# Turning the normed q heads with VectorE instead of TensorE in a one-core decoder layer

## The reference

```python
q, k, v = jnp.split(h @ w_in, 3, axis=-1)
q = rms_norm(split_heads(q, SB_HEADS, SB_HEAD_DIM), q_gain).astype(jnp.float32)
k = rms_norm(split_heads(k, SB_HEADS, SB_HEAD_DIM), k_gain).astype(jnp.float32)
v = split_heads(v, SB_HEADS, SB_HEAD_DIM).astype(jnp.float32)
q = q * (SB_HEAD_DIM ** -0.5)
...
z = jnp.einsum('bhqd,bhkd->bhqk', qb, k)
```

## Time and profile before

| | before |
|---|---|
| median of 3 runs | 1232.27 us |
| profiled execution | 1231.01 us |
| its span | 1229.3 us |
| PE busy | 1221.0 us (99%) |
| DVE busy | 816.4 us (66%) |
| ACT busy | 623.2 us (51%) |
| POOL busy | 79.5 us (6%) |
| granted TensorE clock | 1.00 of full speed in the attention groups |

### The profile page before, as it was taken

One profiled execution on the slowest core, in us unless ns is written; L12 is line 12 of the kernel. 1 busy time (PEld: TensorE's weight loads), 2 busy tenths in 40 slices (PEclk: granted clock), 3 DMA queues, 4 the chain that ended last, 5 costly groups with the idle time before them and its releaser, 6 DMA issues.

```text
span 1229.3 us, 17127 instructions
## 1 busy us (share of the span) xinstructions
PE 1221.0 (99%) x5552; PEld 1013.5 (82%) x5552; DVE 816.4 (66%) x1039; ACT 623.2 (51%) x741; POOL 79.5 (6%) x126
## 2 busy tenths in 40 slices
PE   8999999999999999999999999999999999999998
PEld 7888888888888788888888888888888888888886
DVE  6667577675679866765776676587665656665554
ACT  5458486584945544444444443444444444444443
POOL 0312103121001200000000000000000000002000
PEclk9999999999999999999999999999999999999999
DMA  8655554555555766666666666666565656574674
GB/s 266 204 160 168 171 171 155 179 159 155 172 169 160 220 185 201 193 184 192 203 189 185 205 190 186 200 194 178 190 211 169 213 168 219 164 223 154 198 225 133
DMA packets 120468, 229.33 MB, mean 187 GB/s; under 512 B 7490, under 2 KB 9844, under 8 KB 120436
## 3 DMA queue, kind: packets, MB, share of 16 engines
q1 hardware_dynamic: 119252, 226.80, 59.7%
q10 hardware_dynamic: 1184, 2.11, 0.5%
HBM read 226.78 MB, written 2.10 MB: 186 GB/s over the span
## 4 chain that ended last, share of the span: by engine, by line
PE 98%; DMA 0%; DVE 0%; ACT 0%; issue 0%; SPq 0%; ACTq 0%; DVEq 0%
PE acc L960 95%; PE T L974 1%; PE T L988 1%; PE Z L988 1%; PE R L1011 1%; DMA x<-in_x 0%; PE acc L1072 0%; PE Z L1001 0%; ACT w_hi L406 0%; PE R L1012 0%; DVE stage L924 0%; DVE x L927 0%; DVE neg_log_1m L697 0%; ACT softplus L474 0%; ACT softplus L472 0%
## 5 line engine op out<-in xcount | busy, mean ns | idle before, releaser
L406 ACT ACTIVATE w_hi<-raw 128x1024 fp32r<-128x1024 f32 (+1 forms) x448 | 455.1, 1021 | 523.8 <-PE acc L960 492.3
L644 DVE TENSOR_TENSOR w_lo<-raw,w_hi 128x1024 fp32r<-128x1024 f32 (+1 forms) x448 | 526.5, 1183 | 285.4 <-ACT w_hi L406 279.7
L960 PE MATMUL acc<-w_hi,xT_hi 128*128 128x512 f32 x1216 | 476.9, 392 | 0.2
L960 PE MATMUL acc<-w_hi,xT_lo 128*128 128x512 f32 x1216 | 473.7, 390 | 0.0
L960 PE MATMUL acc<-w_lo,xT_hi 128*128 128x512 f32 x1216 | 473.1, 389 | 0.0
L960 PEld LDWEIGHTS acc<-w_hi,xT_lo 128*128 128x128 f32 x1216 | 228.2, 188 | 48.0
L960 PEld LDWEIGHTS acc<-w_hi,xT_hi 128*128 128x128 f32 x1216 | 228.3, 188 | 46.9 <-issue 1.0
L960 PEld LDWEIGHTS acc<-w_lo,xT_hi 128*128 128x128 f32 x1216 | 228.4, 188 | 46.5
L960 PE MATMUL acc<-w_hi,hT_hi 128*128 128x512 f32 x352 | 136.9, 389 | 0.0
L960 PE MATMUL acc<-w_lo,hT_hi 128*128 128x512 f32 x352 | 136.9, 389 | 0.0
L960 PE MATMUL acc<-w_hi,hT_lo 128*128 128x512 f32 x352 | 136.9, 389 | 0.0
(11 more groups left out here) (124 smaller groups left out, 662.9 us busy)
## 6 DMA issues: line engine op xcount, KB each, us to landing
raw<-in_sb_w_in SPq DMA_DIRECT2D x96, 512.0 KB, 3.7
raw<-in_ffn_w_gate SPq DMA_DIRECT2D x88, 512.0 KB, 3.8
raw<-in_ffn_w_up SPq DMA_DIRECT2D x88, 512.0 KB, 3.8
raw<-in_ffn_w_down SPq DMA_DIRECT2D x80, 512.0 KB, 4.8
raw<-in_sb_w_out SPq DMA_DIRECT2D x32, 512.0 KB, 3.9
raw<-in_ple_w_gate SPq DMA_DIRECT2D x20, 512.0 KB, 4.9
raw<-in_ple_w_gate SPq DMA_DIRECT2D x24, 256.0 KB, 3.5
raw<-in_ffn_w_down SPq DMA_DIRECT2D x16, 256.0 KB, 3.1
```

What stands on the lines that cost most here:

```text
L406: act.activation(w_parts[0][:, slot(u), 0:n, :], raw[:, slot(u), 0:n, :], ACT.Copy).then_inc(hi_ready, 1)
L644: dve.tensor_tensor(w_parts[1][:, slot(u), 0:n, :], raw[:, slot(u), 0:n, :], w_parts[0][:, slot(u), 0:n, :].bitcast(F32), ALU.subtract).th ...
L960: last = pe.matmul(acc[pair][tb][:, :], parts[a][:, c, tb * P:(tb + 1) * P], w_parts[w][:, slot(u), i, :], start=(start and i == 0 and n = ...
```

## The change

The normed q heads no longer go through PE. At u = 14 to 17 DVE turns them itself, four 32x32-block instructions behind each lo, sixteen a group, into a new buffer `q_side` in SBUF; each covers all four heads and both token blocks (eight 32x32 blocks). At u = 18, behind the squares of k, ACT copies `q_side` with the gain to `qT_hi` in one instruction; at u = 19 DVE makes `qT_lo` in one instruction. The k heads stay as they were, and the counts of turn rounds in the waits are lowered from four to two a group. `norm_heads` waits for `q_side_ready` as well, and `scores` for `qT_ready`.

```diff
-    SETS0 = X_ROUNDS + 4 * GROUPS
-    SETS0_T0, SETS0_T1 = (X_ROUNDS + 1) // 2 + 4 * GROUPS, X_ROUNDS // 2
+    SETS0 = X_ROUNDS + 2 * GROUPS
+    SETS0_T0, SETS0_T1 = (X_ROUNDS + 1) // 2 + 2 * GROUPS, X_ROUNDS // 2
+    Q_TURN, Q_UNITS, Q_HI, Q_LO = 14, 4, 18, 19
+            q_side = at_row("q_side", [P, HG, SEQ])
@@ ACT, group
                         if u == end + 3:
                             square_heads(U0 + end, 3 * g + part, 2 * g + part, part)
-                        if u == end + 8:
-                            turn_heads(to, gain, 4 * g + 2 * part, 0)
-
-                        if u == min(end + 10, AU - 1):
-                            turn_heads(to, gain, 4 * g + 2 * part + 1, 1)
+                    if u == Q_HI:
+                        act.wait_ge(q_side_ready, g + 1)
+                        act.activation(qT[0][:, :, :], q_side[:, :, :], ACT.Copy, scale=gains[:, QG:QG + 1]).then_inc(q_hi_ready, 1)
+                    if u == AU - 1:
+                        turn_heads(kT, KG, 2 * g, 0)
+                        turn_heads(kT, KG, 2 * g + 1, 1)
@@ DVE
+            def turn_q(g, i):
+
+                if i == 0:
+                    left(dve, 0, A_P0 + 2 * g + 1)
+                    dve.wait_ge(qT_ready, g)
+                for a, b in QUADRANTS[i * QN * QN // Q_UNITS:(i + 1) * QN * QN // Q_UNITS]:
+                    last = dve.transpose(
+                        q_side[b * Q:(b + 1) * Q, :, :].rearrange("p h (t s) -> p t h s", t=TB)[:, :, :, a * Q:(a + 1) * Q],
+                        normed[a * Q:(a + 1) * Q, :, :].rearrange("p t (h d) -> p t h d", d=HD)[:, :, :, b * Q:(b + 1) * Q])
+                if i == Q_UNITS - 1:
+                    last.then_inc(q_side_ready, 1)
@@ DVE, group
                         if u == end + 6:
-                            norm_heads(2 * g + part, part, 4 * g + 2 * part)
-                        if u == end + 8:
-                            turn_heads(to, gain, 4 * g + 2 * part, 0)
-
-                        if u == min(end + 10, AU - 1):
-                            turn_heads(to, gain, 4 * g + 2 * part + 1, 1)
+                            norm_heads(2 * g + part, part, 2 * g, g + part)
+                    if Q_TURN <= u < Q_TURN + Q_UNITS:
+                        turn_q(g, u - Q_TURN)
+                    if u == Q_LO:
+                        dve.wait_ge(q_hi_ready, g + 1)
+                        dve.scalar_tensor_tensor(out=qT[1][:, :, :], in0=q_side[:, :, :], scalar=gains[:, QG:QG + 1],
+                                                 in1=qT[0][:, :, :].bitcast(F32), op0=ALU.mult,
+                                                 op1=ALU.subtract).then_inc(qT_ready, 1)
+                    if u == AU - 1:
+                        turn_heads(kT, KG, 2 * g, 0)
+                        turn_heads(kT, KG, 2 * g + 1, 1)
@@ PE, group
-                    for i in range(2):
-                        for m in range(2):
-                            if u == (i + 1) * DU + 4 + 2 * m:
-                                left(pe, i, (A_P0 + 2 * g, A_P1 + g)[i] + 1)
-                                turn(0, normed, 2 * m, (X_ROUNDS + 1) // 2 + 4 * g + 2 * i + m)
+                    for m in range(2):
+                        if u == 2 * DU + 4 + 2 * m:
+                            left(pe, 1, A_P1 + g + 1)
+                            turn(0, normed, 2 * m, (X_ROUNDS + 1) // 2 + 2 * g + m)
```

More of the change, by code:

```diff
@@ L203, in trunk @@
         turned_hi = sem("turned_hi")
+        q_side_ready = sem("q_side_ready")
+        q_hi_ready = sem("q_hi_ready")
+        qT_ready = sem("qT_ready")
         side_ready = sem("side_ready")
@@ L513, in group @@
                         attend(u, g - 1, A_EVERY)
-                    for part, (to, gain) in enumerate(((qT, QG), (kT, KG))):
+                    for part in range(2):
                         end = (part + 1) * DU - 1
@@ L665, in sum_heads, with norm_heads @@
                                AX_X).then_inc(head_ssq_ready, 1)
-            def norm_heads(n, pair, rounds):
+            def norm_heads(n, pair, rounds, q_turned):
                 dve.wait_ge(head_scale_ready, n + 1)
                 dve.wait_ge(T_ready, X_ROUNDS + rounds)
+                dve.wait_ge(q_side_ready, q_turned)
                 for tb in range(TB):
@@ L992, in scores @@
             def scores(h, i, g):
-                left_T0 = (X_ROUNDS + 1) // 2 + 4 * (g + 1)
+                left_T0 = (X_ROUNDS + 1) // 2 + 2 * (g + 1)
                 pe.wait_ge(T_free[0], left_T0)
+                pe.wait_ge(qT_ready, g + 1)
                 pe.wait_ge(z_free, h)
```

## The result

| | before | changed |
|---|---|---|
| median, first session (10 and 10 runs) | 1232.1 us (1231.57 to 1233.06) | 1235.9 us (1233.71 to 1238.98) |
| median, second session (16 and 11 runs) | 1232.0 us | 1234.33 us (1232.34 to 1236.53) |
| span of the profiled execution | 1229.3 us | 1234.2 us |
| granted clock of that execution | 0.999 | 0.998 |
| DVE busy | 816.4 us | 842.6 us |

The changed kernel is slower: 1.0032 of before with an interval of 1.0024 to 1.0041 in the first session, 1.0018 (1.0009 to 1.0027) in the second.

The account below looks back on a forecast made before the run. PE was taken to bound the kernel, with 98% of the chain of waits. Losses at the k turn of 1.2 + 3 × 1.6, after PE's saving, gave 6.1 us: 1237.1 profiled, 1238.4 median, range 1230.5 to 1241.

Parts of the forecast that it names:

- My own case: k chain: POOL, held by DVE's row, makes PE wait at the k turn; 6.0 to 6.1 us slower, chance 0.70.
- rival 2: k chain: DVE less late, POOL held once, turn 0.6 us late; 1231.0 us, no change that can be told; chance 0.11.
- PE's rounds: On PE: eight turn rounds go, saving 3.65 us, at least 2.9 and at most 3.9.
- DVE's backlog: DVE, third group: sixteen turns, 7.6 us a group, make `sum_heads` of k start at 211.42, hidden from PE until there.
- POOL held by the row: k chain on POOL: first small operation slips in before `qT_lo`, the second is held by the closed DVE row until 217.5.
- the case I gave beside mine: POOL gets one operation in at each row boundary; k turn at 222.4, 1.2 us lost a group, 4.7 in all.
- The first group: First group's k turn: power held until the lo of u = 21 ends, turn at 70.6 to 70.8; 1.2 us lost.
- The other groups: k turn of the three later groups: PE waits 2.5 us, its saving of 0.89 gone, 1.6 us lost each.
- The sum: Whole kernel: 1.2 + 3 × 1.6 = 6.0 to 6.1 us slower, all else hanging on PE.
- the fall of the clock: Rival 3: clock falls while PE waits, or block turns are dearer and PE waits for lo's; above 1241 us; chance 0.05.
- The signs: Expected in the profile after: second small POOL operation 3 to 4 us, PE waiting 2 to 2.5 us at four k turns.
- Rival 1: k chain: POOL is not held by the row, PE does not wait; 1228.6 us, faster; chance 0.14.

Follow-up runs that it names:

- e5: The changed kernel with one block turn a group instead of sixteen and `qT_lo` made at u = 22: 1227.55 us, 0.9964 of before.
- e2: The changed kernel with `qT_lo` at u = 22 and an idle one-input sum over `q_side` at u = 19: 1227.63 us, 0.9964 of before.
- e10: The changed kernel itself, run again with nothing altered: 1234.33 us, 1.0018 of before.
- e8: The changed kernel with turns at u = 14, 15, 16, 19, `qT_hi` at u = 20, `qT_lo` at u = 22: 1227.78 us, 0.9968 of before.
- e1: The changed kernel with `qT_lo` made at u = 22 instead of u = 19, all sixteen turns kept: 1228.38 us, 0.9967 of before.
- e4: The changed kernel with `qT_lo` made twice in a row at u = 19: 1235.44 us, 1.0032 of before.
- e7: The kernel before with two more powers in POOL's chain for the k factors: 1239.65 us, 1.0063 of before.
- e9: The kernel before with three more powers in POOL's chain for the k factors: 1255.96 us, 1.0180 of before.

## Why the prediction was right, and where its sizes were off

The forecast was slower, 1238.4 us by a wait at the k turn; measured were 1235.9 and 1234.3, both inside the range given. That range was wide, from 1230.5 to 1241. My own case had 1235.5 to 1241 (the 1235.5 stands there without a working; its lowest sum is 1232.3 + 4.7 = 1237.0), and the first median is barely inside that, the second 1.2 us under it. The direction and the mechanism were right; that both medians lie in the range owes something to the room left for rival 2. The replayed clock of the third group can be compared step by step. The changed kernel runs 1.34 later there (its lo of u = 14 starts at 197.84, not 196.50), of which its start and the groups before are the cause; I take this off.

| step | predicted | measured − 1.34 |
|---|---|---|
| `sum_heads` of k starts | 211.42 | 211.35 |
| POOL starts | 212.73 | 212.65 |
| second L363 ends | 217.5 | 216.16 |
| `head_scale` ends | 221.35 | 220.98 |
| PE's k turn | 222.8 | 222.41 |

- **PE's rounds.** Predicted 3.65; by e5, which keeps one block turn a group, 3.64 up to the fourth k turn and 4.3 in the medians. Right in size.
- **DVE's backlog.** Right to 0.1 us. No product waited for a lo.
- **POOL held by the row.** Right in kind: e2 and the rows beside L716 show it. Wrong in detail. I let the first L363 in before L800, since POOL had slipped in before L827, and held the second until 217.5. In the third group the first ended only at 216.28, just after L800. The row was not closed up to the lo of u = 21 either; there was a pause of 0.2 us, and the second L363 came through in it. The fourth group went the same way. In the second group, and in three groups of e10, the first did come in before L800, and the second was held by L800 and the lo of u = 20. The third group here, then the same place in e10:

```profile
213.99 2.29 POOL L363 TENSOR_SCALAR head_ms<-head_ssq,rstd 128x4 f32<-128x4 f32 x1 [18.18 <-DVE head_ssq L670]
```

```profile
213.24 1.17 POOL L363 TENSOR_SCALAR head_ms<-head_ssq,rstd 128x4 f32<-128x4 f32 x1 [18.19 <-DVE head_ssq L670]
214.38 2.29 POOL L363 TENSOR_SCALAR head_ms<-head_ssq,rstd 128x4 f32<-128x4 f32 x1
```

  Either way the power could start only near the end of the lo of u = 21 or after it, and PE waited 1.94 or 1.65. That is the time of the case I gave beside mine, 222.4, but not by its rule of one operation at each boundary: one of the two boundaries around L800 let nothing in. That the time fits is luck in part.
- **The first group.** Predicted 1.2 lost; this is the term that was most wrong. The k turn started at 69.92, with `norm_heads` of q at 45.65 instead of 44.49, as the input came later: 0.36 − 1.16 = −0.80, so most of the saving of 0.98 was kept and PE had no wait there (in e10 it is −0.81). I held the power until the lo of u = 21 was over; it was held by the lo of u = 20 alone:

```profile
64.03 1.21 DVE L650 TENSOR_TENSOR w_lo<-raw,w_hi 128x1024 fp32r<-128x1024 f32 x1
65.65 1.23 DVE L650 TENSOR_TENSOR w_lo<-raw,w_hi 128x1024 fp32r<-128x1024 f32 x1 [0.41 <-ACT w_hi L411]
```

```profile
64.24 2.50 POOL L332 TENSOR_TENSOR head_r<-head_ms,minus_half 128x8 f32<-128x8 f32 x1
```

- **The other groups.** From one first k turn to the next it was 75.82; now 76.79, 77.04 and 77.03: 1.0, 1.2 and 1.2 lost, predicted 1.6 each.
- **The sum.** −0.80 + 1.0 + 1.2 + 1.2 = 2.6 up to the fourth k turn, predicted 6.0; in e10 it is 2.05. The two spans lie 4.9 apart. 1.2 more is the later input, which is chance: `norm_heads` of q starts at 45.65 in this profile and at 44.93 in e10, the same kernel. Up to 5 × (0.32 + 0.03) = 1.75 is the clock. Some 0.6 goes the other way behind the fourth k turn, where e5 and e10 gain 0.9; no term of the prediction has this gain, and its cause is open. I had the fall of the clock as a rival with a small chance. It is no rival but a surcharge, and it came in part of the runs.
- **The signs.** The wait of DVE for POOL (3.58, I had 3 and more) and `head_scale` 9.6 after the sum (I had 9.9) came. The second L363 took 1.25 or 2.29, not 3 to 4, and PE waited three times for up to 1.94, not four times for 2 to 2.5.
- **Rivals 1 and 2** fell as forecasts for this kernel: PE did wait, and the backlog was there. Rival 1 is what e2 and e8 turn the kernel into.

The Trainium skill's rule on two SBUF inputs (SBUF — State Buffer, "Who interferes with whom") holds for e2 in both directions: the lo's held POOL, and the one-input sum of 1.21 us did not. That one operation is let in at the end of each instruction, as "for the whole instruction" might be read, the traces show in some places and not in others: in e1 the first L363 was held for two lo's (2.23), in e4 the power only for one.

## What to carry to other kernels

When work is moved from the bounding engine to another one, the other engine's total time is the wrong question; ask which short chain through a third engine ends next at the bounding one, how much slack it has, and what the new instructions share with it. Here 7.1 us of block turns a group cost nothing once they were spread (e8), and one instruction of 1.3 us in the wrong place cost more than the whole gain. If a chain of small GpSimd operations is waited for, keep VectorE instructions with two SBUF inputs from following each other beside it, or put a one-input instruction between them.

## What the runs showed of the hardware

- POOL's operations on 4 or 8 elements of 0.20 to 0.27 us took up to 2.29 us beside two-input VectorE instructions, and ran at full speed beside a TENSOR_REDUCE of 1.21 us (e2), beside STREAM_TRANSPOSE (e8, the power in 1.65), and beside SCALAR_TENSOR_TENSOR with one input from PSUM and one from SBUF (0.20 each in the changed kernel).
- Not settled: at which boundaries of such a row POOL is let in. In the third group of the two profiles of the changed kernel the same operation came 0.18 us after the lo had started (213.99 − 213.81 and 213.24 − 213.06); it was held for 2.29 us in one and for 1.17 us in the other. So neither the kind of operation nor, to 0.01 us, its moment behind the lo's start decides. What does decide is open.
- Idle PE of up to 1.8 us left the clock alone in all five runs of e7. Of two waits of 1.94 us in the changed kernel's profile one was followed by a fall, one was not. One wait of 2.69 us in e4's profile was not, while in e9 each of four waits of 3.3 to 3.4 us was. So in these rows a longer wait is followed by a fall more often, but 2.69 us need not be; what else decides is not settled.
- A fall cost about 2.5 us beside waits of 3.4 us (e9), and up to 1.75 us beside one of 1.94 us (the changed kernel).
